# A decoder layer on one core: the four engines' head loops written out for all four heads

## What is computed

```python
h = rms_norm(x, norm1_g[l])
qa, ka, va, qb, kb, vb, gb, gate_a, gate_b = jnp.split(h @ w_in[l], split_idx, axis=-1)
qa = apply_rope(rms_norm(qa.reshape(B, S, DA_HEADS, 2, DA_HALF), q_norm_g[l]), positions, ROPE_DIM, ROPE_THETA)
...
oa = rms_norm(diff_attention(qa, ka, va, lam), diff_subln_g[l]) * (1.0 - lam_init)
ya = oa.reshape(B, S, DA_WIDTH) @ w_branch_a[l]
...
ob = retention(qr, kr, vr)
...
yb = (jax.nn.silu(gb) * ob) @ w_branch_b[l]
merged = jax.nn.sigmoid(gate_a) * ya + jax.nn.sigmoid(gate_b) * yb
x = x + merged @ w_out[l]
h2 = rms_norm(x, norm2_g[l])
x = x + hier_moe(h2, w_group_router[l], b_group_router[l], w_expert_router[l], b_expert_router[l],
                 w_gate[l], w_up[l], w_down[l])
```

## Time and profile before

| | |
|---|---|
| median of three runs | 1598.37 us |
| lowest and highest | 1595.57 and 1598.56 us |
| span of the profiled execution | 1595.1 us |
| TensorE matmuls busy | 1459.3 us, 91% |
| VectorE busy | 1135.1 us, 71% |
| ScalarE busy | 744.6 us, 47% |
| GpSimd busy | 376.8 us, 24% |

### The profile page before, as it was taken

The page is one execution under the profiler, slowest core; times in us unless marked ns, Lnnn a source line. Parts: engine busy times, 40 slices in busy tenths (PEclk is TensorE's granted clock), DMA queues, the critical chain, the costliest instruction groups (busy, mean ns, idle before and its releaser), DMA issues.

```text
span 1595.1 us, 20930 instructions
## 1 busy us (share of the span) xinstructions
PE 1459.3 (91%) x7059; PEld 1187.8 (74%) x7060; DVE 1135.1 (71%) x1661; ACT 744.6 (47%) x1034; POOL 376.8 (24%) x453
## 2 busy tenths in 40 slices
PE   4899899899899999999999956999999999999980
PEld 4778788788787766666678845788888888888860
DVE  5876786785785655665573256789888998898865
ACT  5543353353353211111121233777888887877850
POOL 5125324324423300000000001323232223232310
PEclk9999999999999999999999967999999999999995
DMA  5210210210210111122142134999999999999958
GB/s 163 57 41 3 55 40 0 57 40 0 56 41 1 40 40 40 40 59 59 53 157 82 70 132 155 353 372 383 383 384 385 387 384 384 382 386 382 381 212 318
DMA packets 106887, 277.38 MB, mean 174 GB/s; under 512 B 15440, under 2 KB 69712, under 8 KB 82256
## 3 DMA queue, kind: packets, MB, share of 16 engines
q1 hardware_dynamic: 96464, 255.72, 44.2%
q0 software_dynamic: 9216, 16.80, 2.8%
q10 hardware_dynamic: 1152, 4.19, 0.6%
HBM read 268.28 MB, written 25.17 MB: 184 GB/s over the span
## 4 chain that ended last, share of the span: by engine, by line
PE 71%; issue 13%; DVE 5%; POOL 4%; DMA 2%; ACT 1%; SPq 0%; POOLq 0%; DVEq 0%; ACTq 0%
PE proj L85 13%; PE proj L87 13%; PE proj L86 13%; PE scores L85 6%; PE scores L87 6%; PE scores L86 6%; PE scores L743 3%; PE scores L526 2%; PE outs L743 2%; PE turned L743 2%; DMA comb<-y_rows 2%; POOL stats L1175 1%; POOL stats L1192 1%; PE outs L786 1%; PE turned L526 1%
## 5 line engine op out<-in xcount | busy, mean ns | idle before, releaser
L1622 DVE TENSOR_TENSOR w_low<-w_slot,w_high 128x2048 fp32r<-128x2048 f32 x192 | 438.2, 2289 | 68.8 <-ACT w_high L1058 68.2
L1058 ACT ACTIVATE w_high<-w_slot 128x2048 fp32r<-128x2048 f32 x192 | 367.3, 1918 | 118.8 <-DMA w_slot<-in_w_gate 64.1
L85 PE MATMUL proj<-w_high,xeH 128*128 128x512 f32 x512 | 203.0, 396 | 3.0 <-DVE xeL L1643 3.0
L87 PE MATMUL proj<-w_high,xeL 128*128 128x512 f32 x512 | 200.2, 391 | 0.0
L86 PE MATMUL proj<-w_low,xeH 128*128 128x512 f32 x512 | 199.8, 390 | 0.0
L85 PEld LDWEIGHTS proj<-w_high,xeH 128*128 128x128 f32 x512 | 96.9, 189 | 22.8 <-DVE xeL L1643 2.8
L87 PEld LDWEIGHTS proj<-w_high,xeL 128*128 128x128 f32 x512 | 96.4, 188 | 20.6
L86 PEld LDWEIGHTS proj<-w_low,xeH 128*128 128x128 f32 x512 | 96.6, 189 | 19.1
L85 PE MATMUL proj<-wBH,hTH 128*128 128x512 f32 x256 | 108.5, 424 | 0.0
L85 PE MATMUL scores<-w_high,hidH 128*128 128x512 f32 x256 | 103.6, 405 | 3.3 <-DVE hidL L1652 3.3
L1465 DVE RECIPROCAL sig<-sig 128x1024 f32<-128x1024 f32 x16 | 104.9, 6553 | 0.5
(11 more groups left out here) (268 smaller groups left out, 3243.4 us busy)
## 6 DMA issues: line engine op xcount, KB each, us to landing
w_slot<-in_w_gate SPq DMA_DIRECT2D x64, 1024.0 KB, 7.6
w_slot<-in_w_up SPq DMA_DIRECT2D x64, 1024.0 KB, 8.2
w_slot<-in_w_down SPq DMA_DIRECT2D x64, 1024.0 KB, 8.0
wB_in<-in_w_in SPq DMA_DIRECT2D x16, 512.0 KB, 5.8
wC_in<-in_w_in SPq DMA_DIRECT2D x16, 512.0 KB, 5.1
comb<-y_rows SPq DMA_DIRECT2D x16, 512.0 KB, 10.2
wA_in<-in_w_in SPq DMA_DIRECT2D x12, 512.0 KB, 5.8
x_all<-in_x SPq DMA_DIRECT2D x4, 1024.0 KB, 8.0
```

Source lines behind the costliest of these rows:

```text
L85: pe.matmul(out, lh, rh, start=start, stop=False)
L87: return pe.matmul(out, ll, rh, start=False, stop=stop)
L1058: act.activation(w_high[c][:], w_in6[c][:], ACT.Copy).then_inc(S["gu_high" if c < 4 else "d_high"], 1)
L1622: dve.tensor_tensor(w_low[c][:], w_in6[c][:], w_high[c][:].bitcast(F32), ALU.subtract).then_inc(S["gu_low" if c < 4 else "d_low"], 1)
```

## The change

On each of the four compute engines the loop over heads 0 to 2 becomes a Python loop, so that the program holds the round four times, one behind the other. `h` is a number in all of them and `times` returns numbers. SyncE's program is unchanged.

```diff
@@ -709,7 +709,7 @@
             head_steps(0, FILL[:1])
             turn_input(1)
             head_steps(0, FILL[1:])
-            with pe.Fori(0, N_HEADS - 1) as h:
+            for h in range(N_HEADS - 1):
                 head_steps(h, ROUND)
             head_steps(N_HEADS - 1, ROUND, more=False)
             assert not first_pieces
@@ -988,7 +988,7 @@
             act.activation(lam_e, lam_s, ACT.Exp).then_inc(S["lam_expd"], 1)
 
             head_steps(0, FILL[1:])
-            with act.Fori(0, N_HEADS - 1) as h:
+            for h in range(N_HEADS - 1):
                 head_steps(h, ROUND)
             head_steps(N_HEADS - 1, ROUND, more=False)
 
@@ -1201,7 +1201,7 @@
                         pool.tensor_tensor(bstat[:, 9:10], bstat[:, 8:9], mhalf[:, 0:1], ALU.pow).then_inc(S["bn_r"], 1)
 
             head_steps(0, FILL)
-            with pool.Fori(0, N_HEADS - 1) as h:
+            for h in range(N_HEADS - 1):
                 head_steps(h, ROUND)
             head_steps(N_HEADS - 1, ROUND, more=False)
             for i in range(N_TILES):
@@ -1446,7 +1446,7 @@
             dve.tensor_scalar(subln_scaled, subln_col, 1.0 - LAM_INIT, None, ALU.mult).then_inc(S["lam_step"], 1)
 
             head_steps(0, FILL[1:])
-            with dve.Fori(0, N_HEADS - 1) as h:
+            for h in range(N_HEADS - 1):
                 head_steps(h, ROUND)
             head_steps(N_HEADS - 1, ROUND, more=False)
```

## The result

The changed kernel is faster: a median of 1585.93 us against 1597.94, a ratio of 0.9933 with a 95% interval of 0.9914 to 0.9952, so 10.7 us by the ratio (7.7 to 13.7). Its executions took 1583.86 to 1589.92 us; a fifth one, of 2504.99 us at a mean clock of 0.557, is left out of the ratio. The profiled execution is the one with 1589.92 us and a span of 1588.0 us, so 1.8 to 1.9 us lie around a span. The prediction was 1592.2 us, with a range of 1588.3 to 1596.5: the sign and the place were right, the size was too small and the median lies under the range.

A forecast was written before the change was run, and what follows sets the result against it. It took TensorE to bound the head stage, kept waiting in step 3 by VectorE's code refetched after each jump back. 2.34 + 3.32 + 0.03 + 0.45 = 6.14 us off 1598.37 gave 1592.2 us, range 1588.3 to 1596.5.

The forecast's parts named there:

- the two back edges: Jumps back into heads 1 and 2: VectorE's late code delays TensorE in step 3; removing them saves 2.34 and 3.32 us.
- The price of a back edge: Looped step 3 less head 3's straight 6.67 us: 2.34 us into head 1, 3.32 us into head 2.
- The register steps: Register instructions ahead of waits on all four engines go, as head numbers become constants: 0.45 us, ends 0 and 0.9.
- The extra code: Heads 1 and 2 fetched as new code on four engines, hidden behind passes of 125 us: costed at nothing.
- How the sum was set against the runs: Whole kernel: 6.14 us taken from the three-run median 1598.37 gives 1592.2 us; from the span 1595.1, 1588.96.
- The width: Total time: 1.7 us each way for one clock stretch, 1.4 us for run spread, plus the register steps' ends.
- A: VectorE's stall in step 3 stays, only register steps gain: 1597.9 us; chance 0.12 together with its half form.
- half form: The stall into only one of heads 1 and 2 stays: 1594.6 or 1595.6 us; within A's 0.12.
- B: Expert loop's code refetched at each of 28 jumps back: up to 81 us lost, 1673 us; chance 0.05 with C.
- C: New VectorE code late in heads 1 and 2, 2.34 us per place; four give 1601.6 us; chance 0.05 with B.
- D: Half-clock TensorE stretches behind the heads, one more or fewer: 1.7 us, 1590.5 or 1593.9; a width, no own chance.

The follow-up runs named there:

- first set: The changed kernel's first executions, timed against the kernel before: median 1585.93 us against 1597.94, ratio 0.9933; two later sets of the unedited changed kernel both gave 0.9951.
- before again: The kernel before, with no edit, timed against itself: ratio 0.9995, single times 1592.78 to 1598.94 us.
- ScalarE with 298, 346 and 410 instructions: Kernel before with already met waits added to ScalarE's loop body of 185 instructions; steps 3 of heads 1 and 2 took 8.84 to 10.18 us, no total given.
- one jump: Kernel before with VectorE's head 0 as straight code and its loop over heads 1 and 2 only: ratio 0.9981, 3.0 us.
- 367: Kernel before with VectorE norm and rotation work left out, its body refilled with met waits to 367 instructions; such kernels took 2111 to 2121 us, expert routing changed.
- 370: Kernel before with ScalarE's body filled with met waits to 346 instructions, 370 as traced; it stalled after its jump, no total time given.
- 334: Kernel before with VectorE's body shortened to 334 instructions by leaving out norm and rotation work; such kernels took 2111 to 2121 us, expert routing changed.
- 322: Kernel before with ScalarE's body filled with met waits to 298 instructions, 322 as traced; no stall after its jump, no total time given.
- 399: Kernel before with VectorE norm and rotation work left out, its body refilled with met waits to 399 instructions; such kernels took 2111 to 2121 us, expert routing changed.
- 434: Kernel before with ScalarE's body filled with met waits to 410 instructions, 434 as traced; 2.4 us to its next instruction after the jump, no total given.

## Why the prediction was wrong in size

The first median lies 6.3 us under the 1592.2. Of that, 3.3 us is the first set's distance from all 14 executions, for the most part luck, 1.8 us a base that was too high, 0.6 us the clock behind the stalls, and some 0.7 us stays open (rounded). The steps that failed are the base and the width; the mechanism held.

**What bounds, and the two back edges.** Right, by its own steps. Head 3 as a model of the straight heads gave 95.96 us for steps 3 to 15, and the changed kernel has 95.99 and 95.97. The 2.34 and 3.32 us are gone from the steps they were read in (now 6.65 us each).

**The price of a back edge.** This term was too small as an average. It was read from one execution in which one of the two stalls was followed by a stretch at half clock. In the profiles of six kernels that keep VectorE's loop at 391 instructions with two jumps (before, before again, the other three written out, ScalarE with 298, 346 and 410 instructions) nine of the twelve stalls are followed by such a stretch: three show one such stretch and a head stage of 470.1, 470.1 and 470.3 us, and three show two, with 470.7, 471.4 and 471.6 us. Against 464.0 us that is 6.1 to 7.6, 6.7 us on the average.

**The register steps.** 0.45 us with ends 0 and 0.9. In the profiled pair, steps 4 to 14 of heads 0 to 2 went from 268.32 to 267.99 us, 0.33 us less, and with VectorE alone written out the other engines' share of the head stage is 0.3 us. Right.

**The extra code.** Costed at nothing, and nothing it was: 63 code packets in place of 55 on the page, and no step from 3 to 14 of heads 1 and 2 longer than head 3's by over 0.05 us.

**How the sum was set against the runs.** This step failed. 1598.37 us, the median of three runs, was taken as the time to subtract from, with 3.3 us of it "around the span or spread between runs". Time less span is 1.8 us, so the profiled execution took an estimated 1597 us, and 47 executions have a median of 1596.6. So 1.8 us of the distance between 1592.2 and the 14 executions' median of 1589.2 is a base that was too high, 0.6 us is the clock behind the stalls (6.7 - 6.1), and 0.7 us stays.

**The width.** This step failed too. The range allowed 1.7 us for one stretch of clock and 1.4 us for the spread, in both directions. The single times of one kernel turned out to spread over 6 us and more (1592.78 to 1598.94), and the first set's median, 1585.93, lies 3.3 us under the median of all 14. Most of what puts the first result outside the range is that set's luck: its mean clock is 0.9692, against 0.9674 and 0.9666 in the other two. At 0.97 us for each 0.001 that is an estimated 2.1 of the 3.1 us by which the first set's mean lies under that of the other two; the median of all 14 lies inside the range.

**What stays open.** The means differ by 8.2 us, give or take 1.4, and the head stage explains 6.7. In the profiled executions nothing is left for the rest: outside the head stage they take 1125.0 and 1125.1 us in the two of before (1595.1 - 470.1, 1595.2 - 470.1) and 1124.0, 1126.8 and 1124.8 in the three of the changed kernel. The difference of 1.5 us is about as large as its own uncertainty, and without the first set 0.7 us of it are left. A stretch at half clock in the last expert was one candidate. TensorE's window there, in the kernel before and then in the same kernel measured again:

```profile
1544.10:1547.50 3.40, 3.40 (x9) 2.62 (x9) 0.00 (x0) 0.00 (x0) 0.49 (x1) 0.50 0.21 80
```

```profile
1546.00:1549.40 3.40, 3.40 (x10) 2.66 (x9) 0.00 (x0) 0.00 (x0) 0.42 (x1) 0.50 0.21 80
```

It is missing in two of the three profiles of the changed kernel. But these two have another one near 1003 us instead (shown above for the first), so that between the long stretch at half clock of the routing (near 930 us) and the last one the changed kernel has two in each profile, where the kernel before has two and three. It is also missing in one kernel with both jumps (ScalarE with 410). So the profiles speak for no loss of such stretches behind the heads, and the cause of the rest stays open.

**The rivals.** A, the stall stays: no, in any of four profiles without VectorE's long jump. Its half form was made on purpose with one jump, and gave 3.0 us less than before. B, the expert loop loses its residence: no. In 1002 to 1517 of the changed kernel one code packet is moved, where the earlier trace rows have none, and the 28 passes of TensorE's expert loop take 498.6 us, where they took 498.2. C, straight code arrives late: no. D, the clock falls elsewhere: yes, and it was underrated, as it decides more about a single median than the register steps do.

On the code's return, the rule of the Trainium skill's "Runtime: NRT & Kernel Launch", Instruction fetch mechanics, that a taken branch out of the loaded pages waits for a fetch, agrees with the trace. The Trainium skill's "Advanced Engine Details and Errata", ISA Cache, has room for 512 instructions in two lines of 256. The prediction took this for the length of a body that fits, and as such it fails: 367 were too many on VectorE and 370 on ScalarE, while 334 and 322 were kept. The room itself is not refuted: by the estimate above, three pieces of 128 and one fetched ahead are 512. The lines of 256 are not what the packets show, which bring 8192 bytes each. So the two pages are no opposite views, as the prediction had them.

## What to carry to other kernels

In this kernel a hardware loop was free to within 0.3 us as long as its body stayed in what the engine keeps of its code; past that, each jump back cost that engine some 3 us. Whether the kernel pays depends on who waits for that engine. Look at the first instruction of the body for idle time by "issue", and count the body of the engine that shows it: only that engine's loop has to be written out, or its body cut (here 57 instructions fewer were enough). When a gain of under 1% is forecast, take the base from as many executions as there are and put the spread of the clock in the range before anything else: one profile shows one draw of it.

## What the runs showed of the hardware

- A jump back over a body that is too long cost VectorE 2.6 to 3.3 us of idle time (391, 367 and 399 instructions) and ScalarE 2.4 to 2.7 us (370 and 434 as traced); one over a shorter body, nothing that a wait for another engine didn't cover.
- For these bodies, where they stand, the limit is between 334 and 367 instructions on VectorE and between 322 and 370 on ScalarE. With 334 no code packet was moved in two passes; with 367 and 399 there were ten, of 8192 bytes each, and within a pass they came some 128 instructions apart.
- Behind an idle time of TensorE of 2.0 to 2.2 us the granted clock fell to 0.50 (1.2 GHz) for 3.4 us at nine of twelve such places in six profiles, in one execution and not in another at the same place of the same kernel, and cost 1.0 to 1.6 us of step 3 when it did.
- Over 32 executions of one kernel the time went with the mean granted clock, 0.97 us for each 0.001.
